# Mixture-of-experts routing split in two: slot tables of the 32 static blocks ahead of the experts, overflow tables and token weights inside the expert stage

## What is computed

```python
lg = t @ wr_g + br_g;  pg = softmax(lg);  g = argmax(lg)          # 4 groups
le_g = (t @ wr_e + br_e).reshape(n_tok, 4, 8)[group g]
top_v, top_i = top_k(le_g, 2)
weights = (pg[g] * softmax(top_v)).reshape(-1)
expert = g * 8 + top_i                                            # 32 experts
# assignments sorted by expert, padded to blocks, one expert per block
hidden = silu(x_blk @ w_gate[e]) * (x_blk @ w_up[e])
yb = hidden @ w_down[e]
out = zeros.at[buf_tok].add(yb * buf_w)
```

## Time and profile before

| what | us or share |
|---|---|
| median of 3 runs | 2975.8 |
| the profiled execution, device time | 2971.97 |
| its span, first to last instruction | 2970.1 |
| TensorE busy | 2450.8 (83%) |
| VectorE busy | 983.7 (33%) |
| ScalarE busy | 550.3 (19%) |
| GpSimd busy | 166.4 (6%) |
| mean granted TensorE clock | 0.937 |
| gate, up and down loads | 192 of 2048 KB, 35 us from issue to landing |

### The profile page before, as it was taken

How to read it: one execution, slowest core, us unless ns; L and a number is a source line. 1 busy time by engine, 2 the same in 40 slices (tenths; PEclk the granted TensorE clock), 3 DMA queues, 4 the chain that set the end, 5 groups by cost and what they waited for, 6 DMA issues and landing times. The chain is left out here.

```text
span 2970.1 us, 30580 instructions
## 1 busy us (share of the span) xinstructions
PE 2450.8 (83%) x11973; PEld 1304.7 (44%) x11973; DVE 983.7 (33%) x2152; ACT 550.3 (19%) x1220; POOL 166.4 (6%) x273
## 2 busy tenths in 40 slices
PE   6999888784977777497984987777498687999999
PEld 2444366443644333244743653433243553444444
DVE  3211277644222222366734222222264443001000
ACT  3000177220100000014710100000022541000000
POOL 0000000001211111000000211111000000000000
PEclk9999999886999999798996999999799788999999
DMA  8454200507999999510055999999600111221210
GB/s 303 163 192 170 73 1 1 208 30 298 418 419 419 419 418 401 192 43 19 2 193 229 417 418 418 418 418 414 221 32 0 50 72 68 102 85 59 82 57 28
DMA packets 126863, 591.81 MB, mean 199 GB/s; under 512 B 21460, under 2 KB 24028, under 8 KB 71424
## 3 DMA queue, kind: packets, MB, share of 16 engines
q1 hardware_dynamic: 116160, 568.83, 48.3%
q0 software_dynamic: 10560, 21.01, 1.9%
HBM read 579.19 MB, written 24.22 MB: 203 GB/s over the span
## 5 line engine op out<-in xcount | busy, mean ns | idle before, releaser
L1605 PE MATMUL moe_down<-moe_wd,moe_hid_t 128*64 128x512 f32 x1024 | 240.6, 612 | 62.9 <-DMA moe_wd<-in_moe_w_down 50.4
L1579 PE MATMUL moe_up<-moe_wu,moe_xg_t 128*64 128x256 f32 x2048 | 238.1, 385 | 63.2 <-DMA moe_wu<-in_moe_w_up 63.2
L1579 PE MATMUL moe_gate<-moe_wg,moe_xg_t 128*64 128x256 f32 x2048 | 239.5, 387 | 54.4 <-DMA moe_wg<-in_moe_w_gate 52.7
L395 PE MATMUL qkv_acc<-qkv_w,a_buffer 128*128 128x512 f32 x576 | 256.3, 598 | 1.4 <-DVE a_buffer L470 1.2
L2632 PE MATMUL mlp_acc<-m_h,mlp_w 128*128 128x512 f32 x512 | 224.3, 599 | 11.5 <-DMA mlp_w<-in_w_up 9.5
L1579 PEld LDWEIGHTS moe_gate<-moe_wg,moe_xg_t 128*64 128x64 f32 x2048 | 154.1, 139 | 162.0 <-DMA moe_wg<-in_moe_w_gate 91.0
L2647 PE MATMUL mlp_acc<-mlp_w,mlp_u_t 128*128 128x512 f32 x512 | 220.0, 592 | 1.4 <-DVE mlp_u_t L2667 1.4
L1579 PEld LDWEIGHTS moe_up<-moe_wu,moe_xg_t 128*64 128x64 f32 x2048 | 152.9, 138 | 144.5 <-DMA moe_wu<-in_moe_w_up 83.6
L395 PEld LDWEIGHTS qkv_acc<-qkv_w,a_buffer 128*128 128x128 f32 x576 | 107.4, 191 | 132.8 <-issue 124.0
L2632 PEld LDWEIGHTS mlp_acc<-m_h,mlp_w 128*128 128x128 f32 x512 | 97.5, 192 | 137.8 <-issue 127.9
L1665 DVE COPY moe_y<-moe_down 128x512 f32<-128x512 f32 x64 | 44.3, 692 | 342.2 <-PE moe_down L1605 342.2
(11 more groups left out here) (356 smaller groups left out, 2770.0 us busy)
## 6 DMA issues: line engine op xcount, KB each, us to landing
moe_wg<-in_moe_w_gate SPq DMA_DIRECT2D x64, 2048.0 KB, 35.1
moe_wu<-in_moe_w_up SPq DMA_DIRECT2D x64, 2048.0 KB, 34.9
moe_wd<-in_moe_w_down SPq DMA_DIRECT2D x64, 2048.0 KB, 34.9
qkv_mod_w<-in_mod_w SPq DMA_DIRECT2D x48, 1024.0 KB, 5.0
mlp_w<-in_w_up SPq DMA_DIRECT2D x8, 2048.0 KB, 8.6
mlp_w<-in_w_down SPq DMA_DIRECT2D x8, 2048.0 KB, 7.7
qkv_w<-in_a_w_qkv SPq DMA_DIRECT2D x12, 1024.0 KB, 9.5
in_w<-in_w_in SPq DMA_DIRECT2D x4, 2048.0 KB, 19.0
```

The costliest lines, as they stand in the source:

```text
L395: mm = nc.tensor.matmul(acc[i % 4][:], h_t[:, k, t * P:(t + 1) * P], w[:, c % w_ring, k, :], start=(k == 0), stop=(k == KD - 1))
L1579: mm = nc.tensor.matmul(acc[b][halves[f], 0:HF], xg_t[b][:, k, c, :], w[:, c, k, f * HF:(f + 1) * HF], start=(c, k) == (0, 0), stop=(c, k) ...
L1605: mm = nc.tensor.matmul(down[b][halves[c], :], hid_t[:, k, h, :], wd[z][:, 2 * h + k, c * NCHUNK:(c + 1) * NCHUNK], start=(k, h) == (0, 0) ...
```

## The change

- The constants before, iota, rowid, half and a new one, `rev` (descending numbers), are loaded once in `enter_layer_0`, behind rope and ones, in place of four loads at the start of each `route`.
- In `route`, `first_max` takes five steps in place of six, by multiplying the ties with `rev` and taking the largest; the mask of the other groups is two operations in place of twelve; the memsets stand first; the first `where` product waits for `both` alone and not for the running sums.
- The table now has only the 32 static blocks: the one-hot rows take the place of `in_block` and are multiplied with the row numbers while TensorE makes `where`; `lane` compares the rank with 0..63, so assignments of rank 64 and over fall out. The 128 slots are filled by two products of 64 columns each.
- The two exponentials are issued behind `lane`; their sums, reciprocals and products (`token_weights`), the block counts and prefix sums (`count_extra`), the overflow places (`place_extra`) and the overflow table (`list_extra`) go into the expert stage, on VectorE, with the products `collect_extra` on TensorE behind block 1. These write into the unused half of `h_tp`, so TensorE waits for `x_read` before it turns the hidden block of block 2.
- VectorE clears the token buffers in place of GpSimd, and GpSimd waits for that (`cleared`) ahead of its first load. The readers of the count, and GpSimd before block 32's indices, wait for `x_ready`.

```diff
                 s["rope_in"], 16)
-            sp.dma_start(e["ones"][:], e["c_ones"]).then_inc(s["ones_in"], 16)
+            for name in ("ones", "before", "iota", "rowid", "half", "rev"):
...
-            loads = [
-                (before[:], e["c_before"]), (iota[:], e["c_iota"]), (rowid[:], e["c_rowid"]),
-                (half[:], e["c_half"]),
-            ]
-            for dst, src in loads:
-                sp.dma_start(dst, src).then_inc(s["const_in"], 16)
-
             for b in range(1, RING):
...
-
-            pe.wait_ge(s["const_in"], 16 * 4)
-            pe.wait_ge(s["hot_done"], nt + 3)
+            pe.wait_ge(s["zeroed"], 2)
+            pe.wait_ge(s["hot_done"], 1)
             nc.tensor.matmul(where[:], before[:], both[:], start=True, stop=False)
+            pe.wait_ge(s["hot_done"], 1 + nt)
             nc.tensor.matmul(where[:], e["ones"][:], sums[:], start=False, stop=True).then_inc(
                 s["where_done"], 1)
-
-            pe.wait_ge(s["tables_in"], 1)
+            pe.wait_ge(s["what_done"], 2)
             for j in range(2 * nt):
                 a, i = j // nt, j % nt
-                mm = nc.tensor.matmul(slots[:], lane[:, a, i, :], what[:, :, a, i, :],
-                                      start=(j == 0), stop=(j == 2 * nt - 1))
+                if i == 0:
+                    pe.wait_ge(s["lane_done"], a + 1)
+                for side in range(2):
+                    mm = nc.tensor.matmul(slots[HALVES[side]], lane[:, a, i, :], what[:, :, a, i, :],
+                                          start=(j == 0), stop=(j == 2 * nt - 1))
             mm.then_inc(s["slots_done"], 1)
...
+            def first_max(hot_out, best, place, values, scratch, order):
...
+                link(v.tensor_tensor(scratch, values, inner(best, values.shape[2]), ALU.is_equal))
+                link(v.tensor_tensor(scratch, scratch, middle(order, nt), ALU.mult))
+                link(v.tensor_reduce(place, scratch, AX.X, ALU.max))
+                link(v.tensor_tensor(hot_out, scratch, inner(place, values.shape[2]), ALU.is_equal))
...
+            by_group = lambda ap: ap.rearrange("p t (g x) -> p t g x", g=NG)
+            v.memset(both[:, nt, :], 0.0).then_inc(s["zeroed"], 1)
+            v.memset(sums[:, 0, :], 0.0).then_inc(s["zeroed"], 1)
+            first_max(hot_g[:], row(0), row(1), lg, tied_g[:], rev[:, 0:NG])
+            link(v.tensor_scalar(away[:], hot_g[:], -1.0, -NEG, ALU.add, ALU.mult))
+            link(v.tensor_tensor(by_group(le[:]), by_group(lge), over(away[:], EPG), ALU.add))
+            first_max(hot[:, 0], row(2), code[:, 0], le[:], tied[:], rev[:, NG:])
+            link(v.scalar_tensor_tensor(le[:], hot[:, 0], 2 * NEG, le[:], ALU.mult, ALU.add))
+            first_max(hot[:, 1], row(3), code[:, 1], le[:], tied[:], rev[:, NG:])
+            v.tensor_tensor(both[:, 0:nt, :], hot[:, 0], hot[:, 1], ALU.add).then_inc(
...
+                v.tensor_tensor(what[:, z], hot[:], over(ids, NE), ALU.mult).then_inc(
+                    s["what_done"], 1)
+
+            dve.wait_ge(s["where_done"], 1)
+            link(v.tensor_tensor(mine[:], hot[:],
+                                 where[:, 0:nt, :].unsqueeze(1).broadcast_to([P, 2, nt, NE]), ALU.mult))
+            link(v.tensor_reduce(rank[:], mine[:], AX.X, ALU.add))
+            for a in range(2):
+                v.tensor_tensor(lane[:, a], middle(iota[:, 0:TB], nt), inner(rank[:, a], TB),
+                                ALU.is_equal).then_inc(s["lane_done"], 1)
+            v.tensor_tensor(r["tg"][:], lg, inner(row(0), NG), ALU.subtract).then_inc(s["gexp_in"], 1)
+            v.tensor_tensor(r["gap"][:], row(3), row(2), ALU.subtract).then_inc(s["wexp_in"], 1)
+            v.tensor_copy(r["held"][:], where[:, nt, :])
             dve.wait_ge(s["slots_done"], 1)
-            link(v.tensor_scalar(r["index"][:, :, 0:nb], slots[:], half[:], None, ALU.add))
-            link(v.memset(r["index"][:, :, nb:], int(BIG)))
+            v.tensor_scalar(r["index"][:, :, 0:NE], slots[:], half[:], None, ALU.add)
...
             for b in range(2):
-                nc.gpsimd.memset(xg[b][:], 0.0).then_inc(s["cleared"], 1)
-                pool.wait_ge(s["cleared"], b + 1)
                 gather(b, b, b + 1)
             for i in range(NE):
                 b = i % 2
                 pool.wait_ge(s["turned_x"], i + 1)
+                if i == NE - 2:
+                    pool.wait_ge(s["x_ready"], 1)
...
-            def one_block(i, b, turn, spare, z, fill):
+            def collect_extra():
+
+                pe.wait_ge(s["x_tables_done"], 2)
+                pe.wait_ge(s["read_h"], 2)
+                for j in range(2 * nt):
+                    a, i = j // nt, j % nt
+                    for side in range(2):
+                        mm = nc.tensor.matmul(x_slots[HALVES[side]], lane[:, a, i, :],
+                                              what[:, :, a, i, :], start=(j == 0),
+                                              stop=(j == 2 * nt - 1))
+                mm.then_inc(s["x_slots_done"], 1)
+
+            def one_block(i, b, turn, spare, z, fill, collected=True):
                 pe.wait_ge(ring["g_in"][z], 16 * fill)
                 pe.wait_ge(s["read_x"], i + 1)
...
+                if collected:
+                    pe.wait_ge(s["x_read"], 1)
...
-                one_block(i, i % 2, i // 2, i >= 2, i % RING, i // RING + 1)
+                one_block(i, i % 2, i // 2, i >= 2, i % RING, i // RING + 1, i >= 2)
+                if i == 1:
+                    collect_extra()
...
+            def token_weights():
+                group, one = chosen[:, 0], chosen[:, 1]
+                link(v.tensor_reduce(group, r["tg"][:], AX.X, ALU.add))
+                link(v.reciprocal(group, group))
...
+
+            def count_extra():
+
+                link(v.tensor_scalar(held_i[:], r["held"][:], float(TB - 1), None, ALU.add))
+                link(v.tensor_single_scalar(held_i[:], held_i[:], 6, ALU.arith_shift_right))
...
+                    a = 1 - a
+                link(v.tensor_tensor(later[:], end[a][:], blocks[:], ALU.subtract))
+                link(v.scalar_tensor_tensor(later[:], later[:], float(NE - 1), iota[:, 0:NE], ALU.add,
+                                            ALU.subtract))
+                return end[a]
...
+            def place_extra():
+
+                link(v.tensor_scalar(first[:], r["code"][:], -1.0, float(NE), ALU.mult, ALU.add))
+                link(v.tensor_tensor(mine[:], r["hot"][:],
+                                     later[:].unsqueeze(1).unsqueeze(1).broadcast_to([P, 2, nt, NE]),
...
+                link(v.scalar_tensor_tensor(more[:], dest_f[:, 1], 0.0, more[:], ALU.is_gt, ALU.mult))
+                link(v.tensor_tensor(first[:], first[:], more[:], ALU.add))
+                link(v.tensor_tensor(dest_f[:, 1], dest_f[:, 1], first[:], ALU.add))
+                link(v.tensor_tensor(lane[:],
+                                     iota[:, 0:TB].unsqueeze(1).unsqueeze(1).broadcast_to(
+                                         [P, 2, nt, TB]), over(dest_f[:, 0], TB), ALU.is_equal))
+                link(v.tensor_tensor(in_block[:],
+                                     iota[:, NE:nb].unsqueeze(1).unsqueeze(1).broadcast_to(
+                                         [P, 2, nt, nx]), over(dest_f[:, 1], nx), ALU.is_equal))
+                for z in range(2):
+                    ids = e["rowid"][:, z:z + 2, tiles[0]:tiles[0] + nt]
+                    v.tensor_tensor(what[:, z], in_block[:], over(ids, nx), ALU.mult).then_inc(
+                        s["x_tables_done"], 1)
...
+            def list_extra(last):
+                dve.wait_ge(s["x_slots_done"], 1)
+                v.tensor_scalar(r["index"][:, :, NE:nb], x_slots, e["half"][:], None,
+                                ALU.add).then_inc(s["x_read"], 1)
+                link(v.memset(r["index"][:, :, nb:], int(BIG)))
+                link(v.tensor_tensor(past[:], middle(last[0:1, :], nx), inner(iota[0:1, 0:nx], NE),
+                                     ALU.is_le))
+                link(v.tensor_reduce(expert_f[:], past[:], AX.X, ALU.add))
+                link(v.tensor_scalar(expert_f[:], expert_f[:], float(NE - 1), None, ALU.min))
+                link(v.tensor_copy(r["expert"][:], expert_f[:]))
+                link(v.tensor_copy(r["count"][:], last[0:1, NE - 1:NE]))
+                dve.wait_ge(s["x_read"], 1)
+                dve.sem_inc(s["x_ready"], 1)
+
             def one_block(i, b, spare):
                 dve.wait_ge(s["expd"], i + 1)
                 nc.vector.tensor_scalar(sig[:], sig[:], 1.0, None, ALU.add).then_inc(s["step"], 1)
...
+            for b in range(2):
+                v.memset(xg[b][:], 0.0).then_inc(s["cleared"], 1)
+            token_weights()
+            last = count_extra()
             for i in range(NE):
                 one_block(i, i % 2, i >= 2)
+                if i == 0:
+                    place_extra()
```

(2 more changed lines are left out.)

202 lines of the change are left out of this document (80 added, 122 removed).

## The result

The changed kernel took 2938.2 us, the median of 4 runs (2935.62 to 2939.4), beside 2976.02 for the kernel before (4 runs, 2970.79 to 2979.58): a ratio of 0.9875, 95% interval 0.9859 to 0.989, so 1.1 to 1.4% faster. Forecast were 2942 us and a range of 2934 to 2958.

The account below looks back on a forecast made before the run. The prediction took weight transfers to bound the expert stages, so the first refill's start counts. Gains of 17.8 us (layer 0) and 14.8 (layer 1) made 32.6, giving 2939.4 or 2943.2 by baseline; it forecast 2942 us, range 2934 to 2958.

Parts of the forecast that it names:

- What bounds the stage, and where the gain lands: Expert stages: weight transfers bound them at 16.2 us a block, so an earlier first refill ends the stage earlier.
- VectorE's chain: Routing, layer 0: shorter operations and no wait for constants let slot products start at about 677.6 instead of 700.00.
- The slot products: Routing on TensorE: 48 narrower products take 6.7 us in layer 0, and layer 1's take 4.9.
- The hand-over and the landing: Layer 0: 2.3 us from slot products to token load, then 15.1 to first refill, including 3.7 for slower landing.
- the upper bound of 19.5: Layer 0's first refill: largest gain expected, with slot products of 5.1 us; the forecast gain was 17.8.
- Layer 1's cap: Layer 1: the refill queues behind slot 2's load until 1610.7, limiting the gain to about 14.8 us, bounds 12 to 15.5.
- Work inside the stage at nothing: Expert stage: moved work makes TensorE 5.4 to 7.2 us late from block 2, covered by queued transfers; layer 0 margin under 3.
- One of my own signs of a wrong prediction: Expert stage: a clock below 1.00 at block 2 was listed as showing the prediction wrong.
- The rival in which it stays down: Expert stages: the clock falls to 1.2 GHz and stays, blocks take about 21 us, total 3003 us; chance 0.03.
- The port rule: Routing: if every narrow VectorE row blocked GpSimd's descriptors, the load would wait for the chain; saving 23, not 32.6 us.
- The sum: Whole kernel: 17.8 us from layer 0 plus 14.8 from layer 1, 32.6 us saved.
- The start of the program at nothing: Program start: five constant loads ahead of modulation slices 8 to 10 take 2.3 us to issue, costed nothing, at most 1.

Follow-up runs that it names:

- e2: Changed kernel with about 6.4 us (as planned) of idle VectorE work added to layer 0's routing chain alone; 2940.56 us, ratio 0.989.
- e7: Changed kernel with slot products taking all 128 lanes at once, 24 instead of 48 products in layer 0; 2941.57 us, ratio 0.9895.
- e11: Changed kernel with slot products reordered, all of the first 64 lanes and then all of the second, instead of alternating; 2937.5 us, ratio 0.9883.
- e10: Changed kernel with the overflow loop skipped when empty, and the first token load waiting only for its own buffer's clearing; 2929.72 us, ratio 0.9856.
- e3: Changed kernel with about 6.4 us (as planned) of idle VectorE work added to layer 1's routing chain alone; 2939.01 us, ratio 0.9884.
- e4: Changed kernel with about 13.5 us (as planned) of idle VectorE work added to layer 1's routing chain alone; 2946.86 us, ratio 0.991.
- e5: Changed kernel without the counting, placing, collecting and listing of overflow blocks inside the expert stage; 2939.66 us, ratio 0.9883.
- e6: Changed kernel with about 8.2 us (as planned) of idle VectorE work behind the overflow placing in both layers' expert stages; 2946.48 us, ratio 0.9913.
- e1: Kernel before with only its five constant tables loaded once at program start instead of four in each routing stage; 2964.55 us, ratio 0.9968.

## Why the prediction was right, point by point

- **What bounds the stage, and where the gain lands: right.** Path idle before the first refill, then full; block pitch and transfer rate unchanged; the gain moved through the stage to its end in both layers, and e2 shows it one for one.
- **VectorE's chain: right.** The slot products were forecast to start 10.8 us after the stage's start and did so after 10.95; in layer 1, 8.7 and 9.0.
- **The slot products: the term that was mis-sized.** "48 x 5.10/24 x 0.66 = 6.7 us" measured 2.83, in layer 1 1.98 instead of 4.9. Two things were wrong. The factor 0.66 came from the mean duration of one weight load, which is the time from start to end of loads that overlap; the price of a narrow product is about half of a wide one (e7 and e11 in layer 1). And the sum had no term for two products that run beside each other because they write the two halves of the output by turns; by e11 that is what made 2.83 of some 5. The lower bound of 5.1, "if only the column count mattered", would have fitted products that don't alternate.
- **The hand-over and the landing: near.** The token load came 2.7 us behind the slot products (forecast 2.3; the clearing of both buffers holds it). From the load to the first refill 15.6 us passed (forecast 15.1). So the first refill of layer 0 stood at 32.1 for "35", and layer 0 gained 20.7 for 17.8, more than the upper bound of 19.5. It could gain no more: with only 0.6 us of dip left in the path, e10's and e11's changes at the refill no longer showed at the end.
- **Layer 1's cap: right, and the size almost exact** (14.9 for 14.8; the terms as written, 1623.7 + 2.1 - 1610.7, add up to 15.1). The faster slot products raised the refill's lead to 17.9, and the cap took 3.0 of it; e3 and e4 found the same 2.5 to 3.0.
- **Work inside the stage at nothing: right** (e5), with the margin near where it was put (2.4 us in layer 0, by e6). The sig of block 1 stood 14.4 us behind that of block 0 (700.68 and 715.10), as forecast. `collect_extra` took 1.58 us, not 3.3 to 5.1: alternating narrow products again, at the high clock.
- **The clock.** One of my own signs of a wrong prediction did show: 1.2 GHz around 720. It cost 1.7 us of down product, inside the margin, and was back at 0.96 in the microsecond from 723. The rival in which it stays down (3003 us) did not come about.
- **The port rule, as the prediction spelled it out: not borne out.** The first token load was issued in 1.20 us with narrow rows of VectorE beside it (the memsets had ended at 683.67), the second in 1.02; before, 1.19 and 1.04. The rule of the Trainium skill (SBUF — State Buffer, Who interferes with whom) says that copies, casts and scalar operations can block GpSimd for their whole length. If every narrow row did so in turn, the load would have waited for the chain; here the trace shows no such wait, and the measured 35.6 us speaks against the 23 of that rival.
- **The sum.** 32.6 forecast, 35.6 measured in the marks, 37.8 in the medians; the difference lies in layer 0 and is the slot products. By size of the parts: constants about 7 (e1), the rest, some 29, the shorter table work. The time was 3.8 us under the forecast, inside the range. Some luck is in that: the gain passed the sum of the upper bounds (19.5 + 15.5 = 35.0), and the time stayed above 2934 because that end was counted from a low execution, 2971, and not from the median.
- **The start of the program at nothing: not contradicted.** SyncE issued the slices 2.7 us later (41.90 against 39.22), TensorE used them at 52.00 instead of 50.81, with no wait on a transfer. In the twelve profiled kernels with the constants at the start, layer 0's `route` began between 664.85 and 668.15 us, against 666.72 before: a cost of some microseconds is not seen, one under the drift of the phases is not excluded.
